# Moving fp32r operands of a transformer kernel to other distances modulo 128 words

## The reference

```python
    for l in range(DEPTH):
        xn = rmsnorm(h, g_mix[l])
        proj = xn @ w_in[l]
        ...
        h = h + jnp.concatenate([hm, ha], axis=-1) @ w_out[l]
        h = h + memory_cross_attention(rmsnorm(h, g_cross[l]), rmsnorm(mem, g_mem[l]),
                                       w_xq[l], w_xk[l], w_xv[l], w_xo[l])
        h = h + peer_ffn(rmsnorm(h, g_ffn[l]), w_pq[l], sub_keys1[l], sub_keys2[l],
                         expert_down[l], expert_up[l])
```

```python
    for layer in range(DEPTH_2):
        hn = rms_norm(h, mix_norm_g[layer])
        ...
        h = h + mix.astype(h.dtype)
        hn = rms_norm(h, ffn_norm_g[layer])
        h = h + conv_ffn(hn, ffn_w_up[layer], ffn_conv_w[layer], ffn_conv_b[layer], ffn_w_down[layer]).astype(h.dtype)
```

## Time and profile before

| | us |
|---|---|
| median of 3 runs | 1698.1 |
| lowest, highest | 1697.87, 1701.24 |
| the profiled execution | 1698.76 |
| its span, from the first to the last instruction | 1696.9 |

### The profile page before, as it was taken

One profiled execution on the slowest core, in us unless ns is written; L12 is line 12 of the kernel. 1 busy time (PEld: TensorE's weight loads), 2 busy tenths in 40 slices (PEclk: granted clock), 3 DMA queues, 4 the chain that ended last, 5 costly groups with the idle time before them and its releaser, 6 DMA issues.

```text
span 1696.9 us, 30404 instructions
## 1 busy us (share of the span) xinstructions
PE 1671.6 (99%) x12006; PEld 1552.6 (91%) x12006; DVE 1232.3 (73%) x1848; ACT 951.0 (56%) x1182; POOL 364.7 (21%) x417
## 2 busy tenths in 40 slices
PE   8899999999999999999999999999999999999999
PEld 8899999999999999988888887999999788899987
DVE  6775467999998666666666666887788555768873
ACT  7865555545555555544544444785555456555552
POOL 0000000003767776201001000000355000005530
PEclk9999999999999999999999999999999999999999
DMA  8345253676556555777777776533455543345552
GB/s 305 135 146 182 108 177 129 228 237 215 187 179 194 187 187 190 269 243 231 239 239 235 236 241 226 216 125 132 177 190 176 197 173 126 125 174 177 194 190 110
DMA packets 73949, 323.48 MB, mean 191 GB/s; under 512 B 8679, under 2 KB 8935, under 8 KB 55888
## 3 DMA queue, kind: packets, MB, share of 16 engines
q1 hardware_dynamic: 58880, 285.24, 48.9%
q0 software_dynamic: 5568, 19.38, 3.7%
q10 hardware_dynamic: 9360, 16.92, 2.7%
HBM read 303.68 MB, written 17.83 MB: 189 GB/s over the span
## 4 chain that ended last, share of the span: by engine, by line
PE 71%; DVE 14%; issue 5%; ACT 4%; POOL 4%; DMA 1%; POOLq 0%; SPq 0%; DVEq 0%; ACTq 0%
PE bank L602 10%; PE bank L604 10%; PE bank L603 10%; PE bank L982 7%; PE bank L984 7%; PE bank L983 7%; PE bank L935 5%; PE bank L939 5%; PE bank L938 5%; DVE lo_u L2266 3%; DVE wlo L1891 3%; POOL upad L533 3%; PE bank L947 2%; DVE oh L2277 2%; ACT whi L1330 1%
## 5 line engine op out<-in xcount | busy, mean ns | idle before, releaser
L1564 ACT ACTIVATE hi_u<-raw_u 128x1024 fp32r<-128x1024 f32 x256 | 272.0, 1063 | 283.2 <-PE bank L982 167.9
L1891 DVE TENSOR_TENSOR wlo<-raw,whi 128x2048 fp32r<-128x2048 f32 x137 | 314.9, 2298 | 103.9 <-PE bank L602 75.3
L1330 ACT ACTIVATE whi<-raw 128x2048 fp32r<-128x2048 f32 x137 | 262.9, 1919 | 70.1 <-PE bank L602 64.9
L935 PE MATMUL bank<-xh,hi_u 128*128 128x256 f32 x1024 | 292.0, 285 | 1.3 <-DVE lo_u L2266 1.0
L2266 DVE TENSOR_TENSOR lo_u<-raw_u,hi_u 128x1024 fp32r<-128x1024 f32 x192 | 238.3, 1241 | 70.8 <-PE bank L935 62.5
L938 PE MATMUL bank<-xl,hi_u 128*128 128x256 f32 x1024 | 285.6, 279 | 0.0
L939 PE MATMUL bank<-xh,lo_u 128*128 128x256 f32 x1024 | 285.4, 279 | 0.0
L602 PE MATMUL bank<-nh,whi 128*128 128x256 f32 x904 | 256.7, 284 | 1.7 <-DVE wlo L1891 0.9
L497 POOL TENSOR_SCALAR oh<-kept,sel_T 128x128 f32<-128x128 f32 x256 | 198.9, 793 | 254.8 <-ACT sel_T L1614 170.4
L603 PE MATMUL bank<-nl,whi 128*128 128x256 f32 x904 | 252.9, 280 | 0.0
L604 PE MATMUL bank<-nh,wlo 128*128 128x256 f32 x904 | 252.7, 280 | 0.0
(11 more groups left out here) (404 smaller groups left out, 3497.3 us busy)
## 6 DMA issues: line engine op xcount, KB each, us to landing
raw<-in_weights SPq DMA_DIRECT2D x138, 1024.0 KB, 4.8
raw_u<-in_experts SPq DMA_DIRECT2D x256, 512.0 KB, 4.1
aside<-a_out ACTq DMA_DIRECT2D x64, 256.0 KB, 3.4
a_in<-aside POOLq DMA_DIRECT2D x64, 256.0 KB, 3.6
const<-in_const SPq DMA_DIRECT2D x1, 1409.0 KB, 9.8
const<-in_const POOLq DMA_DIRECT2D x1, 1409.0 KB, 6.3
h<-in_x SPq DMA_DIRECT2D x2, 512.0 KB, 5.2
raw<-in_weights SPq DMA_DIRECT2D x4, 256.0 KB, 6.7
```

The source lines that it names most:

```text
L935: mm = pe.matmul(out, w[0][:, kp], xh[:, k, :], start=(k == 0), stop=False)
L1330: a(A(whi[:, n % HIGH, :], raw[:, n % RAW, :], ACT.Copy), S("weights_hi"))
L1564: a(A(hi_u[:, u % HIGH_U, :], raw_u[:, u % RAW_U, :], ACT.Copy), S("unit_high"))
L1891: v(V.tensor_tensor(wlo[:, n % LOW, :], raw[:, n % RAW, :], whi[:, n % HIGH, :].bitcast(F32), ALU.subtract), S("weights_split"))
```

## The change

`Area.beside(at, by)` moves a cursor forward until its remainder modulo 128 is that of `at + by`. It is used ahead of memh, ahead of nh1, and for four pairs of tiles that take the place of nh2, one for each of norms 4 to 7, which overlap in one region (40, -24, 24 and -40 words from `HIGH_AT`). gh and gl get a pair for each layer (24 and 80 words). The regions grow by 128 words (112 for `HALVES_END`), and what follows them shifts. No instruction is added, removed or moved in its queue. The diff:

```diff
--- before.py
+++ after.py
@@ -216,6 +216,10 @@
 
             def __init__(self, at):
                 self.at = at
+
+            def beside(self, at, by):
+
+                self.at += (at + by - self.at) % 128
 
             def __call__(self, name, *shape, dt=F32):
                 self.at = -(-self.at // 8) * 8
@@ -264,7 +268,7 @@
         ident = cst("ident")
 
 
-        HALVES_END = 48592
+        HALVES_END = 48704
         crossed = Area(ARENA)
         kxT = crossed("kxT", KD, T)
         vx = crossed("vx", TB, D)
@@ -272,6 +276,7 @@
         memx = m1("memx", TB, D)
         qkpad = m1("qkpad", 4, T + 3)
         wT = Area(crossed.at)("wT", 8, 384)
+        m1.beside(HIGH_AT, -24)
         memh = m1("memh", KD, T, dt=F32R)
         meml = m1("meml", KD, T, dt=F32R)
         qkT = m1("qkT", 4, T)
@@ -318,9 +323,10 @@
         pos = p3("pos", 8, 16, dt=U32)
         posab = p3("posab", 2, 8, 16, dt=U32)
         posf = p3("posf", 2, 8, 16)
+        p3.beside(HIGH_AT, -24)
         nh1 = p3("nh1", KD, T, dt=F32R)
         nl1 = p3("nl1", KD, T, dt=F32R)
-        assert p3.at == HALVES_END
+        assert p3.at <= HALVES_END
         ef = p3("ef", TB, 2, 8, 16)
         gate = p3("gate", TB, P)
 
@@ -361,10 +367,13 @@
 
             return lo_u[:, (u + 1) % LOW_U, :] if u <= P else lo_up[:, :] if u % 2 else lo_u[:, 0, :]
 
-        block2 = Area(BLOCK2)
-        nh2 = block2("nh2", KD, T, dt=F32R)
-        nl2 = block2("nl2", KD, T, dt=F32R)
-        ARENA2 = block2.at
+
+        halves_of = []
+        for n_, by in ((4, 40), (5, -24), (6, 24), (7, -40)):
+            block2 = Area(BLOCK2)
+            block2.beside(HIGH_AT, by)
+            halves_of.append((block2(f"nh{n_}", KD, T, dt=F32R), block2(f"nl{n_}", KD, T, dt=F32R)))
+        ARENA2 = BLOCK2 + 2 * KD * T + 128
         e4 = Area(ARENA2)
         ev = [None] * 7
         for i in (0, 1, 3, 4, 2, 5, 6):
@@ -384,9 +393,13 @@
 
         rW = Area(XH)("rW", 4, 384)
 
-        f5 = Area(ARENA2)
-        gh = f5("gh", 22, T, dt=F32R)
-        gl = f5("gl", 22, T, dt=F32R)
+        f5 = Area(ARENA2 + 128)
+        gated_of = []
+        for layer_, by in ((0, 24), (1, 80)):
+            halves = Area(ARENA2)
+            halves.beside(HIGH_AT, by)
+            gated_of.append((halves(f"gh{layer_}", 22, T, dt=F32R), halves(f"gl{layer_}", 22, T, dt=F32R)))
+        f5.at += 2 * 22 * T
         upad = f5("upad", 2, T + 2)
         fc = f5("fc", 2, T)
         fs = f5("fs", 2, T)
@@ -414,7 +427,7 @@
         og = Area(ARENA2)("og", TB, D)
 
 
-        normed = {0: (xh, xl), 1: (memh, meml), 2: (nh1, nl1), 3: (nh1, nl1), 4: (nh2, nl2), 5: (nh2, nl2), 6: (nh2, nl2), 7: (nh2, nl2)}
+        normed = {0: (xh, xl), 1: (memh, meml), 2: (nh1, nl1), 3: (nh1, nl1), 4: halves_of[0], 5: halves_of[1], 6: halves_of[2], 7: halves_of[3]}
         gains = {0: "g_mix", 1: "g_mem", 2: "g_cross", 3: "g_ffn", 4: None, 5: "ffn0", 6: "mix1", 7: "ffn1"}
 
         def gain(n, k):
@@ -1143,7 +1156,7 @@
                                     norm_T(6, h, q)
                             for k in range(2):
                                 kk = 2 * i + k
-                                mm = three(banks[2 * half + tb][:, :], [x[:, kk, tb * P:(tb + 1) * P] for x in (gh, gl)],
+                                mm = three(banks[2 * half + tb][:, :], [x[:, kk, tb * P:(tb + 1) * P] for x in gated_of[layer]],
                                            [p[:, k, half * 512:(half + 1) * 512] for p in w], kk == 0, kk == 21)
                             if i == 10:
                                 cur["b"] = of[2 * half + tb]
@@ -1732,9 +1745,9 @@
                     a(A(fs[:, s, :], fc[:, s, :], ACT.Silu), S("u_silu"))
                     if m:
                         drained(up, m - 1)
-                        a(A(gh[:, m - 1, :], gated[:, (m - 1) % 2, :], ACT.Copy), S("gated_high"))
+                        a(A(gated_of[layer][0][:, m - 1, :], gated[:, (m - 1) % 2, :], ACT.Copy), S("gated_high"))
                 drained(up, 21)
-                a(A(gh[:, 21, :], gated[:, 1, :], ACT.Copy), S("gated_high"))
+                a(A(gated_of[layer][0][:, 21, :], gated[:, 1, :], ACT.Copy), S("gated_high"))
                 for i in range(1, 11):
                     point(SLOT_OF[f"down{layer}"] + i)
 
@@ -2469,7 +2482,8 @@
 
                 def low(m):
                     dve.wait_ge(S("gated_high"), 22 * layer + m + 1)
-                    v(V.tensor_tensor(gl[:, m, :], gated[:, m % 2, :], gh[:, m, :].bitcast(F32), ALU.subtract), S("ffn_gated"))
+                    high, rest = gated_of[layer]
+                    v(V.tensor_tensor(rest[:, m, :], gated[:, m % 2, :], high[:, m, :].bitcast(F32), ALU.subtract), S("ffn_gated"))
 
                 point(SLOT_OF[up])
                 inv_root(5 + 2 * layer)
```

## The result

| | before | after |
|---|---|---|
| median of 7 runs each, us | 1698.10 (1697.73 to 1701.24) | 1703.64 (1701.72 to 1705.43) |
| ratio, 95% interval | | 1.0026 [1.0016, 1.0036] |
| profiled execution, span, us | 1696.9 | 1701.8 |
| predicted, us | | 1691.9 (1682 to 1701) |

The two medians differ by 5.5 us (0.33%), the spans of the two profiled executions by 4.8 us; the ratio of 1.0026 corresponds to 4.4 us. The forecast had the sign wrong and the range does not hold the time. What came is rival 3, "the even and odd stages lose their good level", while the stages that were to gain got a pitch (the time from one start of a matmul to the next) between the old 120 ns and the hoped-for 113.3.

The account below looks back on a forecast made before the run. TensorE (PE), busy 99% of the span, was taken as the bound, with a matmul pitch set by address distance. Gains of 0.7 + 0.6 + 1.3 + 2.1 + 0.4 + 1.1 = 6.2 us off 1698.1 gave 1691.9 us, range 1682 to 1701.

Parts of the forecast that it names:

- rival 3: Even and odd stages lose their good level at distances 88 and 104: 5.7 us lost there, 1705 us in all; chance 0.13.
- I take 113.3: Pitch assumed for 256-column matmuls at the new distances 24, 88 and 104: the lowest, most stable fp32r level, 113.3 ns.
- xk, xv, xq, pq: Product stages ahead of the even stage: pitch falls from about 120 to 113.3 ns, gaining 0.7, 0.6, 1.3 and 2.1 us.
- even and odd: Two stages already at 113.2 ns except one chunk each near 118; gain 0.4 us.
- up1: Up stage of norm 7: covered by the 5.73 us loop, so 0; at pitch 120 a loss of 0.03 us per chunk.
- down slots 3 to 10: Down stages of both layers, 512 columns: 384 matmuls at 231.1 instead of 234.0 ns, gain 1.1 us.
- The factor of 2/3: Share of the even and odd stages where PE was taken to set the pace, used to price changes there.
- The loop of 5.73 us: Up stages: a turn over ACT, POOL and DVE takes 5.73 us, covering 48 matmuls (5.66 us), so gain 0.
- The marks named beforehand: Expected: xq 179 matmuls in 20 us, even 232 in 26, up turn 5.73 us, down slots 4 to 10 5.55 us.
- Rival 1: No collision at offsets not multiples of 16: pitches 109 and 218 ns, gain 17.3 us, 1680.8 us; chance 0.14.
- Rival 2: Distances act smoothly, or not at all because the stage makes the level: 1698 to 1699.5 us; chance 0.25.
- Rival 4: Expert products, 3072 matmuls, have their levels drawn anew: 1 to 2 us either way; no chance of its own.

Follow-up runs that it names:

- all16: The changed kernel with every moved distance set to 112 (16 for memh as weights): 1696.54 us, ratio 0.9983 to the kernel before.
- down0: The kernel before's distances, with only gh of the down slots moved to distance 0 in both layers: 1696.82 us, ratio 0.9985 to the kernel before.
- undo46: The changed kernel with norms 4 and 6 alone put back to distance 112: 1698.45 us, ratio 1.0000 to the kernel before.
- chi64: The kernel before with chi, clo, g_final and lo_up 16 words higher, chi and clo at distance 64 instead of 80: 1692.66 us, ratio 0.9962.
- undo467: The changed kernel with norms 4, 6 and 7 put back to their old distances (112, 112, 16): 1699.38 us, ratio 0.9999 to the kernel before.

## Why the prediction was wrong, point by point

**The step that failed** is "I take 113.3: ... it is reached at 112, the row nearest to 104". Nothing of the table above runs smoothly from neighbour to neighbour: 48 has the lowest of the 256-column levels and 40, one step of 8 words away, has 117.3 or 118.7 and never 113.3. Modulo 64 the new distances 88 and 24 are the same one, 24, and it is as bad as 0; 104 is 40. In place of 113.3 the runs gave 118.7 at 104 in xq and up0, 118.0 in odd, 120.0 at 88 in even and up1, and 119.9 at 24 in xv. I had no row at any of them, and the rows I had were all at multiples of 16. Of the six distances seen with 256 columns three had given 120 and three 113 or 118 (counted by the ten rows of 256 columns in the earlier trace rows), so a new one had an even chance of the better kind at most, and of 113.3 throughout a smaller one; I also took "levels seem to be discrete" as speaking against a loss. The levels are discrete, but there are more of them than the three that I had seen: 116.6, 117.3, 118.3 and 118.7 came with the new distances.

**Terms of the sum.** What was forecast, and what the table of starts shows:

| term | forecast, us | measured, us |
|---|---|---|
| xk, xv, xq, pq | -4.7 | -1.5, of which about -1.0 not by the addresses (and +0.3 ahead of xk) |
| even and odd | -0.4 | +5.0 |
| up0 | 0 | 0 |
| up1 | 0, or +0.03 a chunk at a pitch of 120 | +1.2 |
| down slots 3 to 10 | -1.1 | +0.2 in down0; -0.5 around slot 3 of down1 |
| experts and the rest | 0, 1 to 2 either way | +0.2 |

- *xk to pq.* The places were right (PE sets the pace there) and the size was off: 1.3 ns per matmul, 120.0 to 118.7, instead of 6.7, and no gain in xv, 119.9 both times. 4.7 x 1.3/6.7 = 0.9. What came by the addresses is 189.3 - 188.8 = 0.5.
- *even and odd.* Rival 3 had the mechanism, and nearly the price: 5.7 us for the two, where 5.0 came. The factor of 2/3 for where PE sets the pace has no working in the prediction. In the even stage it was about right: the mean pitch rose by 6.2 ns over 656 differences, 4.1 us, and the stage by 3.0. In the odd stage it was not: the mean pitch rose by 4.0 ns over 506 differences, 2.0 us, and all of it came. That the odd stage's price, 2.6, is near the 2.0 is luck: a rise put too high and a factor put too low. Its condition was right: the new level had to be above about 116, and it was 120.0 and 118.0.
- *up.* The loop of 5.73 us was right, and it was the most useful reading of the profile. It hides 118.7 (nothing lost in up0), it nearly hides 114.0 (0.3 us won in all16), and it does not hide 120.0. I had priced the last case at 0.03 us a chunk, 0.65 for one stage; it was 1.2, since PE begins the stage behind the loop and has nine chunks to catch up in, which the prediction did not see.
- *down.* The slots that count were the right ones, as down0 shows (2.1 us from 384 matmuls). The value taken, 231.1, belonged to distance 80; 104 gives 234.2 and 48 gives 233.3. Again a neighbour's value was given to a distance that has its own.

**The marks named beforehand.** xq was to count 179 matmuls in 20 us and counts 170; it is not at 120 but hardly off it. The even stage was to keep 232 in 26 us and has 211 in 25, which would be 219 in 26: the mark "even and odd rise above 116 ns" is met, and it was the one that decides. The down slots 4 to 10 were to take 5.55 us and take 5.62 in down0 and 5.60 in down1. The turn of the up loop was to stay at 5.73 us, and does: 1232.68 - 1226.95. ACT in up0 of the kernel after:

```profile
1226.95 0.42 ACT L1745 ACTIVATE fs<-fc 128x256 f32<-128x256 f32 x1 [2.46 <-DVE fc L2507]
...
1232.68 0.42 ACT L1745 ACTIVATE fs<-fc 128x256 f32<-128x256 f32 x1 [2.46 <-DVE fc L2507]
```

**Rivals.** Rival 1, no collision at an offset that is no multiple of 16, with 109 and 218, is out: 24 and 40 gave 120.0 and 118.7, and the lowest level of unbroken stretches is 113.3 to 113.5 in every one of the twelve kernels here. For 512 columns a level of 227 exists that I had not seen, but 218 was never reached, and 227 is at a multiple of 64. Rival 2 had two halves. Its levels, 117 at 104 and 118.5 at 88, were the nearest of all forecasts for 104 (118.7, and 117.3 by turns in odd) and too low for 88 (120.0); its reason, a smooth function, is wrong. Its other half, that the stage and not the address makes the level, fell with undo46, all16 and chi64, in each of which stages changed their pitch when addresses alone had changed; in undo46 it was the two stages whose norms were moved, while xq, xv and up1 kept 118.7, 119.9 and 120.0. With it goes the rule of the Trainium skill, "TensorE: Matmul & The Clock Gate", Part 2, step-by-step, that the moving operand and the weight load read SBUF through independent ports and loading takes nothing from the running matmul: here the same instructions took 113.3 or 120 ns, and 226.8 or 231.1, by the distance between the two addresses, so the trace disagrees on the second half of it; whether the ports are independent it cannot show. Rival 4 was real: 0.6 us in after, and 1.4 of the 2.5 us by which undo467 is later than undo46 at the even stage, enough to hide the 1.2 us that the latter was built to show.

**The chances.** The even and odd stages already stood at the best level that the trace had, so of all places they could only lose, and they hold 1248 matmuls, against the 720 in xk to pq on which the gain rested. To give a loss there 0.13 and 0.48 to the case that every new distance hits the best level was not borne out by the rows, none of which lay at a new distance.

## What to carry to other kernels

Where PE is busy 99% of the time, divide the length of unbroken stretches by their count: a matmul's shown duration, its waits and its idle time did not show that one stage ran 6% slower than another. For fp32r with a new weight load per matmul, fix the distance between stream and next weights on purpose, modulo 64 words, and measure each value: 48 had the lowest level for 256 columns (beside 117.8), 0 was best for 512, and each is near the worst for the other. Before pricing such a gain look for a loop over other engines with a fixed turn, since it sets a threshold: all pitches below it are worth nearly the same, and the first one above it costs. See also whether PE starts the stage behind the loop and needs its faster pitch to catch up.

## What the runs showed of the hardware that was not expected

- The pitch depends on the distance modulo 64 words (256 bytes), and distances 8 words apart already differ (113.3 at 48, 117.3 at 40). Where the pair lies did not matter: moved together by 8 words, the counts stayed identical (169 in xq, 232 in the even stage).
- Matmuls of 256 and 512 columns want different distances. Distance 0 gives the slowest 256-column level, 120.0 (as 24 does), and the fastest 512-column one, 227.
- At distances 16 and 48 there are two levels, 113.3 and 117.8, for the same instructions. One holds as long as PE is not interrupted, 431 matmuls in a row in the experts' part of the kernel before, and a pause may change it. What draws it was not found. It moves a stage from kernel to kernel though its distance is the same: the experts' 256-column part took 421.4 to 423.6 us in the twelve profiles, the even stage 97.1 to 98.4 at distance 112. It is why an effect of 1 us has to be read from its own stage and not from the total.
- The Trainium skill, "TensorE: Matmul & The Clock Gate", "Back-to-back issue gap", gives N/2.4 + 2.5 ns for the isolated gap from one matmul to the next, 109.2 for 256 and 215.8 for 512 columns. The best levels seen here were 113.3 and 226.7, 4 and 11 ns above it.
- Why these distances collide, and with which of the two weight loads, was not settled.
